# One 1 MB transfer for two weight units in place of a 512 KB transfer for each, in a two-layer decoder kernel

## The reference

```python
for layer in range(DEPTH):
    i = layer // 2
    if layer % 2 == 0:
        h = h + even_mixer(rmsnorm(h, even_mix_norm[i]), even_w_in[i], ...)
    else:
        h = h + odd_mixer(rmsnorm(h, odd_mix_norm[i]), pos, odd_w_in[i], odd_w_out[i])
    h = h + memory_cross_attention(rmsnorm(h, xattn_norm[layer]), rmsnorm(mem, mem_norm[layer]),
                                   xattn_wq[layer], xattn_wkv[layer], xattn_wo[layer])
    h = h + swiglu(rmsnorm(h, ffn_norm[layer]), ffn_w_gate_up[layer], ffn_w_down[layer])
return rmsnorm(h, final_norm)
```

## Time and profile before

| | us |
|---|---|
| median of 3 runs | 1392.5 |
| lowest, highest | 1392.46, 1392.71 |
| the profiled execution | 1392.8 |
| its span, first to last instruction | 1391.1 |
| PE busy in the span | 1379.7 |
| DVE, ACT, POOL busy | 890.0, 640.9, 108.0 |

### The profile page before, as it was taken

One profiled execution on the slowest core, in us unless ns is written; L12 is line 12 of the kernel. 1 busy time (PEld: TensorE's weight loads), 2 busy tenths in 40 slices (PEclk: granted clock), 3 DMA queues, 4 the chain that ended last, 5 costly groups with the idle time before them and its releaser, 6 DMA issues.

```text
span 1391.1 us, 20695 instructions
## 1 busy us (share of the span) xinstructions
PE 1379.7 (99%) x8090; PEld 1214.9 (87%) x8090; DVE 890.0 (64%) x1240; ACT 640.9 (46%) x953; POOL 108.0 (8%) x90
## 2 busy tenths in 40 slices
PE   9999999999999999999999999999999999999997
PEld 8988888888999998888877788988888999998887
DVE  6656556479888883334578755765559887885332
ACT  6632534354545552322756635544454545554221
POOL 0012200110000000100211211100020000000000
PEclk9999999999999999999999999999999999999999
DMA  9721320222323233333221212542131332323321
GB/s 349 260 91 61 106 91 31 91 91 83 116 92 122 92 108 129 100 117 138 96 87 48 85 35 79 191 139 77 46 107 60 122 114 99 108 106 121 106 76 61
DMA packets 42136, 147.16 MB, mean 106 GB/s; under 512 B 5056, under 2 KB 5568, under 8 KB 42048
## 3 DMA queue, kind: packets, MB, share of 16 engines
q1 hardware_dynamic: 38448, 136.46, 28.6%
q10 hardware_dynamic: 3600, 9.45, 1.9%
HBM read 143.80 MB, written 2.10 MB: 105 GB/s over the span
## 4 chain that ended last, share of the span: by engine, by line
PE 96%; DVE 2%; issue 1%; ACT 1%; DMA 0%; POOLq 0%; POOL 0%; ACTq 0%; DVEq 0%
PE acc L1851 19%; PE acc L1853 19%; PE acc L1852 19%; PE acc L2189 8%; PE acc L2190 7%; PE acc L2191 7%; PE acc L1899 3%; PE acc L1901 3%; PE acc L1900 3%; PE aux L2191 1%; PE aux L2190 1%; PE aux L2189 1%; PE acc L2269 1%; PE aux L2257 1%; PE aux L1853 0%
## 5 line engine op out<-in xcount | busy, mean ns | idle before, releaser
L1131 DVE TENSOR_TENSOR w_lo<-raw,w_hi 128x1024 fp32r<-128x1024 f32 x181 | 224.9, 1244 | 215.0 <-ACT w_hi L578 214.4
L578 ACT ACTIVATE w_hi<-raw 128x1024 fp32r<-128x1024 f32 x181 | 190.0, 1053 | 185.2 <-PE acc L1853 146.4
L1851 PE MATMUL acc<-act_hi,w_hi 128*128 128x512 f32 (+1 forms) x374 | 141.6, 379 | 0.0
L1853 PE MATMUL acc<-act_hi,w_lo 128*128 128x512 f32 (+1 forms) x374 | 140.9, 377 | 0.0
L1852 PE MATMUL acc<-act_lo,w_hi 128*128 128x512 f32 (+1 forms) x374 | 140.9, 377 | 0.0
L1851 PE MATMUL acc<-u_hi,w_hi 128*128 128x512 f32 x352 | 138.7, 394 | 0.0
L1853 PE MATMUL acc<-u_hi,w_lo 128*128 128x512 f32 x352 | 137.2, 390 | 0.0
L1852 PE MATMUL acc<-u_lo,w_hi 128*128 128x512 f32 x352 | 137.1, 389 | 0.0
L1056 POOL TENSOR_TENSOR sqsum<-sqsum,tmp 128x512 f32<-128x512 f32 x41 | 53.2, 1297 | 978.2 <-ACT tmp L587 978.2
L2189 PE MATMUL acc<-b_hi,w_hi 128*128 128x256 f32 x432 | 122.6, 284 | 1.4 <-issue 1.4
L2189 PE MATMUL acc<-b_hi,s_hi 128*128 128x256 f32 x432 | 122.3, 283 | 0.0
(11 more groups left out here) (251 smaller groups left out, 3220.4 us busy)
## 6 DMA issues: line engine op xcount, KB each, us to landing
raw<-in_weights SPq DMA_DIRECT2D x253, 512.0 KB, 3.3
hT<-in_x_t ACTq DMA_DIRECT2D x4, 512.0 KB, 7.3
x_tok<-in_x ACTq DMA_DIRECT2D x4, 512.0 KB, 5.2
raw<-in_weights SPq DMA_DIRECT2D x5, 256.0 KB, 5.8
mem_tok<-in_mem ACTq DMA_DIRECT2D x2, 512.0 KB, 5.8
out_h<-out_f SPq DMA_DIRECT2D x2, 512.0 KB, 2.6
memT<-in_mem_t SPq DMA_DIRECT2D x3, 256.0 KB, 6.0
out_h<-out_tok ACTq DMA_DIRECT2D x1, 640.0 KB, 3.7
```

The lines of the kernel that those rows point to most:

```text
L578: act.activation(w_hi[:, s, :], raw[:, s, :], ACT.Copy).then_inc(hi_ready, 1)
L1131: dve.tensor_tensor(w_lo[:, s, :], raw[:, s, :], w_hi[:, s, :].bitcast(F32), ALU.subtract)\
L1851: pe.matmul(out, w_h, x_h, start=first, stop=False)
L1853: return pe.matmul(out, w_l, x_h, start=False, stop=last)
```

## The change

From unit 4 on, SP's loop body of four waits and four transfers of one unit becomes two waits and two transfers of two units. A pair (n, n+1), n even, goes to slots 0 and 1 or 2 and 3. Its one semaphore is that of the even slot. SP waits until `w_lo` of unit n-3 is made, since both slots have to be free. Those who waited for `raw_in` of a unit now wait for `landed(n)`: for units 0 to 3 their own semaphore, later that of the even slot of the pair, with the same count. DVE's pair sums wait once and no longer twice.

```diff
+        def landed(n):
+
+            return raw_in[n % RING if n < RING else n % RING // 2 * 2]
...
             with sp.Fori(1, UNITS // RING) as i:
-                for j in range(RING):
-
-                    sp.wait_ge(lo_ready, i * RING + (j - RING + 1))
-                    sp.dma_start(raw[:, j, :], d["weights"][bass.ds(i * RING + j, 1)].rearrange("a p n -> p (a n)"))\
+                for j in range(0, RING, 2):
+
+                    sp.wait_ge(lo_ready, i * RING + (j - RING + 2))
+                    sp.dma_start(raw[:, j:j + 2, :], d["weights"][bass.ds(i * RING + j, 2)].rearrange("a p n -> p a n"))\
                         .then_inc(raw_in[j], 16)
...
-                act.wait_ge(raw_in[s], lin(16 * (n // RING + 1), i, 16))
+                act.wait_ge(landed(n), lin(16 * (n // RING + 1), i, 16))
...
-                    act.wait_ge(raw_in[n % RING], 16 * (n // RING + 1))
+                    act.wait_ge(landed(n), 16 * (n // RING + 1))
...
-                    dve.wait_ge(raw_in[x], 16 * (n // RING + 1))
-                    dve.wait_ge(raw_in[y], 16 * (n // RING + 1))
+                    dve.wait_ge(landed(n), 16 * (n // RING + 1))
```

## The result

The changed kernel takes 1401.39 us in the median of 4 runs (1401.20 to 1402.57), the kernel before 1392.57 us (4 runs, 1392.46 to 1392.71). The ratio is 1.0063, with a 95% interval of 1.0051 to 1.0075. It is slower by 8.8 us, three times the 0.2% that the prediction called distinguishable. The prediction of 1392.7 us, and its range up to 1395.3, were wrong. Of all executions in this document one is left out, a slow one (1700.3 us at a granted clock of 0.75, of the kernel with pairs from unit 16 on).

The account below looks back on a forecast made before the run. PE was taken to bound the kernel, busy 1379.7 of 1391.1 us. Removed work was worth 0 and start stalls 0.2 us, so the 1392.5 us median became 1392.7, range 1392.0 to 1395.3.

Parts of the forecast that it names:

- the signs of being wrong: ACT starting unit 4 after 16.7 us, a PE gap at 35 us, or any gap in the pairs or near 890 us.
- the stretch near 890 us: Second projection of the memory, 870 to 915 us: tightest stage after the start, cover 2.2 us, cost 0.
- Units 4 and 5: At the start: issued at 10.58 us, both land at about 15.65, cover 0.34 us before PE needs unit 4.
- Rival 2: At the saturated start: first 1 MB transfer lands late, at 18.8 us or later; slower by over 2.8 us; chance 0.09.
- Units 6 and 7: At the start: issued at 15.47 us, down at 20.77, `w_lo` of unit 6 ready at 23.1, cover 0.65 us.
- the sum: Three places at the start with 0.3 to 0.7 us of cover: 0.2 us of stall in all, added in full.
- Units 10 and 11: At the start: issued at 25.4 us, down at 30.9, cover 0.7 us; with `hT` loads up to 2.6 us later.
- Rival 1: At the start: one of three covers breaks, most easily at units 10 and 11; stall 1 to 2.8 us; chance 0.13.
- the halves and the eviction: Behind the landing of units 10 and 11: 2.33 us until `w_lo` is made and 0.7 us for an eviction.
- The stages behind: After the start: feed-forward pairs, second projection of the memory and the other stages each cost 0.
- 7.4 + 1.3: Worst-traffic bound for 1 MB, 8.7 us: longest 512 KB transfer, 7.4, plus 1.3 for a further 512 KB.
- the same: Whole kernel: time not distinguishable from before, within 0.2% or 2.8 us; chance 0.87.

Follow-up runs that it names:

- the run on DVE's order: The changed kernel, but DVE evicts two `xv` tiles before the split of unit 10 and the last `xk` before that of unit 18: 1398.05 us.
- the run with the zero matmuls: The changed kernel with seven more zero matmuls of 128 columns on a spare bank ahead of unit 10 on PE: 1401.56 us.

## Why the prediction was wrong, step by step

**The signs.** Of the signs of being wrong that the prediction named, one came: PE's gap at 35 us. ACT starts unit 4 at 15.80, and the pairs and the stretch near 890 us have no gap.

**Units 4 and 5: right.** Landing and split were put at 15.65 and came at 15.78 and 15.80. The 5.0 us from issue to landing held exactly (5.1 to 5.4 in the traces of the five other kernels with this joint transfer), and so did counting bytes where the engines are saturated (389 GB/s from 7 to 20 us, and 401 before). Rival 2, a first landing at 18.8 or later, did not happen; its sign was right, by another mechanism.

**Units 6 and 7: right in this trace, and by luck.** Put at 20.77, landed at 21.50, 5.9 us after the issue where 5.3 was put. The cover had been put at 0.65 us; PE's weight loads wait 0.3 us for `w_lo` at 23.9, and its matmuls run from 20 to 33 us without a gap. The same joint transfer took 6.6 to 7.8 us in the traces of the five other kernels that have it, and in each PE waited 0.3 to 1.1 us for `w_lo` of unit 6. So this cover did break there, and each of these stalls alone is more than the 0.2 us that the sum had for all places.

**Units 10 and 11: the step that failed.** It said "The backlog is gone by then, so 5.5 us, down at 30.9", and put 0.7 us of cover behind it. The issue came at 26.00 (25.4 put), and the landing at 35.35. The term of 5.5 us measured 9.35. The working had named the `hT` loads, but as a bound of 2.6 us more, and that bound counted their bytes alone. The trace shows that bytes are not all: from 26 to 28 us, with this transfer under way, the engines moved 188 GB/s, and 401 from 30 to 32. Why they moved so little is open. The working also didn't follow the consequence of its own claim that both units land together: the pair 8 and 9 then lets ACT run through two splits and put out two `hT` loads 0.46 us apart, just ahead of this transfer. That the bunching matters is argued: with the two loads 2.05 us apart (units 10 and 11 alone in a pair) the transfer still took 7.8 us. With three `hT` loads moved behind it, it takes 4.9 us, so the value of 5.5 would have held there. Rival 1 named the place, "most easily at units 10 and 11", and had 0.13 and up to 2.8 us. The place was right and the price too small.

**What the stall costs once it is there: missing.** The sum took a late landing as a stall of the same length, once. For the first stall that holds: 35.35 and the 3.03 us that the working had for the halves and the eviction give 38.4, and PE goes on at 38.50. But that stall is 2.9 of the 8.3 us. Two things were left out. DVE regains at most 0.4 us a unit, so a lateness of 8 us is not gone by the next tight place. And the granted clock falls to 0.50 behind a gap of 2.9 us, which lengthens PE's busy time, on which the prediction says nothing. "PE never waits for anything else that could take it up" was right, and it also holds for what is added.

**The place at 60 us: not looked at.** The start was costed up to unit 11. Units 18 and 19 meet the four `x_tok` loads, 7.4 us. On time that is free (the run with pairs from 16 on has 6.5 us there and no wait); 8 us late PE stalls for 2.1 us. The joint transfer is not needed for that: with pairs for units 4 to 15 alone, units 18 and 19 come singly and PE loses 2.8 us there, to a DVE that is late and busy without a gap.

**The stages behind: right.** The 18 pairs of each feed-forward part, the second projection of the memory, and all others cost 0, as the run with pairs from 16 on shows. The median of 4.9 us for 1 MB lies in the bounds of 4.6 to 8.7 us, and the maximum of 9.4 above them: 7.4 + 1.3 was no upper end.

The Trainium skill, "DMA: Bandwidth & Descriptors", section Bandwidth, gives 6.15 us for 1 MB, for transfers that the general engine issues. The trace, with transfers issued by SP, differs on both sides: 4.9 us in the median, and 9.35 us where a second queue has loads of its own under way. By its figure the landing of units 10 and 11 would be 32.2 us, an estimate, and the stall would be missed all the same.

**The chances.** 0.87 stood on "the same". The three covers were 0.3 to 0.7 us, and each landing depended on the one before it, so their failures were not independent. The table shows 3.35 us for the parts and 6.8 for the whole.

## What to carry to other kernels

A ring that is filled in larger pieces loses nothing where there is stock, and loses first where all queues start together: follow every step there until the stock is full, and past each further load of another queue, not only to the first tight place. Two units that land together also make their reader run twice in a row, and everything that reader issues goes out in a bunch; ask what that meets (how much the bunching itself cost here is not shown). Where covers are a few tenths and each landing depends on the last, cost them as a chain: separate losses of 1.1, 1.9 and 0.35 us gave 6.8 together. A time inside the expected range does not prove its reason: look for the wait that the reason says must go.

## What the runs showed of the hardware

The granted clock fell behind PE gaps of 2.9, 3.9 and 4.0 us: it reads 0.50 (1.2 GHz) in the 6 us behind the first, and 0.62 and 0.57 in the 8 us in which the two others end. Behind gaps of 1.5 us (in three kernels) and of 2.1 us it reads 1.00. The length of one gap is not all: in the run on DVE's order PE stood still for 1.00 and for 0.68 us just before 7.45 us, with 4 short matmuls between, and the clock read 0.62 and 0.53 from 7 to 9 and from 9 to 11 us. In the run with pairs from unit 10 to 15, gaps of 0.8 and 0.7 us at the same place left it at 1.00.

One transfer's time. The same 1 MB, units 10 and 11 with `hT` loads beside it, took 6.1, 6.2, 7.6, 7.8 and 9.35 us from issue to landing in five traces, issued at 23.10, 23.45, 23.43, 23.47 and 26.00 us. Two issues 0.02 us apart differ by 1.4 us. In three more traces it took 7.8 (issued at 26.60, with two `hT` loads 0.45 us apart at the same moment), 6.7 and 5.7 us. And one transfer was slow with the engines nearly free: in the run with the zero matmuls, units 8 and 9 took 9.2 us (19.48 to 28.7), though from 24 to 26 us the engines were busy for 0.23 and moved 45 GB/s. The kernel's time scatters with it: 1393.4 to 1401.6 us for pairs from unit 10 on, where the kernel before lies within some tenths in nearly all runs. What decides between the shorter and the longer landing was not settled.
